# Two transformer blocks on one core: latent and grouped heads of the first mixer divided before their product, and their products written transposed

## What is computed

```python
# 6 latent heads, width 64; 4 differential heads, width 128; 6 grouped heads, width 64
p = softmax(q @ k.T * scale)          # latent and grouped heads: o = p @ v
a = softmax(s0) - lam * softmax(s1)   # differential heads: o = rms_norm(a @ v)
mix = concat([o_latent, o_diff, o_grouped], axis=-1)    # 256 x 1280
x = x + mix @ w_o
```

## Time and profile before

| | before |
|---|---|
| median of 3 runs | 2326.1 us |
| profiled execution | 2325.82 us, of which the span is 2323.9 us |
| TensorE busy | 2224.8 us, 96% |
| VectorE / ScalarE / GpSimd busy | 1693.7 / 1476.0 / 227.8 us |
| mean granted TensorE clock | 0.982 |
| attention steps 8 to 22, first layer | about 105 to 184 us from the span's start |
| the same, second layer | about 472 to 551 us |

### The profile page before, as it was taken

The page is one execution under the profiler, slowest core; times in us unless marked ns, Lnnn a source line. Parts: engine busy times, 40 slices in busy tenths (PEclk is TensorE's granted clock), DMA queues, the critical chain, the costliest instruction groups (busy, mean ns, idle before and its releaser), DMA issues.

```text
span 2323.9 us, 31037 instructions
## 1 busy us (share of the span) xinstructions
PE 2224.8 (96%) x11606; PEld 1882.1 (81%) x11606; DVE 1693.7 (73%) x2409; ACT 1476.0 (64%) x2139; POOL 227.8 (10%) x138
## 2 busy tenths in 40 slices
PE   8889999889999999999999899999999999999997
PEld 7777888787887898788888788888888888888885
DVE  6845556864556546655655699999999999999998
ACT  6654445664444465444466488777878787888886
POOL 1420000331001250100242000000000000000000
PEclk9999999999999999999999799999999999999999
DMA  7425555414554643655544399999999999999996
GB/s 285 136 72 182 189 187 191 151 59 153 189 187 159 213 145 129 207 184 190 200 150 148 110 341 367 351 365 348 366 353 370 350 369 348 370 365 373 367 372 240
DMA packets 157275, 570.89 MB, mean 246 GB/s; under 512 B 18560, under 2 KB 18912, under 8 KB 156480
## 3 DMA queue, kind: packets, MB, share of 16 engines
q1 hardware_dynamic: 154032, 555.58, 67.7%
q0 software_dynamic: 3088, 13.27, 1.6%
HBM read 567.72 MB, written 1.05 MB: 245 GB/s over the span
## 4 chain that ended last, share of the span: by engine, by line
PE 72%; DVE 4%; ACT 1%; issue 1%; POOL 0%; DVEq 0%; POOLq 0%; ACTq 0%
PE bank L500 20%; PE bank L502 19%; PE bank L501 19%; PE bank L2035 3%; PE bank L2036 2%; PE bank L2037 2%; PE bank L1661 1%; DVE w_lo L441 1%; PE bank L1003 1%; PE bank L2601 1%; PE bank L1018 1%; DVE X L1919 1%; PE bank L945 1%; PE bank L2532 0%; DVE X L1878 0%
## 5 line engine op out<-in xcount | busy, mean ns | idle before, releaser
L441 DVE TENSOR_TENSOR w_lo<-raw,w_hi 128x1024 fp32r<-128x1024 f32 x990 | 1193.2, 1224 | 299.0 <-ACT w_hi L435 268.5
L435 ACT CAST w_hi<-raw 128x1024 fp32r<-128x1024 f32 x1055 | 1101.0, 1051 | 321.8 <-PE bank L502 269.1
L500 PE MATMUL bank<-w_hi,x_hi 128*128 128x512 f32 (+2 forms) x2144 | 838.7, 391 | 23.4 <-DVE x_lo L1943 7.9
L502 PE MATMUL bank<-w_hi,x_lo 128*128 128x512 f32 (+2 forms) x2144 | 826.1, 385 | 0.0
L501 PE MATMUL bank<-w_lo,x_hi 128*128 128x512 f32 (+2 forms) x2144 | 825.9, 385 | 0.0
L500 PEld LDWEIGHTS bank<-w_hi,x_hi 128*128 128x128 f32 x2144 | 406.7, 190 | 102.1 <-POOL w_lo L441 8.5
L502 PEld LDWEIGHTS bank<-w_hi,x_lo 128*128 128x128 f32 x2144 | 405.9, 189 | 79.6
L501 PEld LDWEIGHTS bank<-w_lo,x_hi 128*128 128x128 f32 x2144 | 406.9, 190 | 73.3
L441 POOL TENSOR_TENSOR w_lo<-raw,w_hi 128x1024 fp32r<-128x1024 f32 x65 | 154.6, 2382 | 576.4 <-ACT w_hi L435 571.5
L502 PE MATMUL bank<-w_hi,qk_l 128*128 128x512 f32 (+1 forms) x496 | 191.4, 386 | 0.0
L500 PE MATMUL bank<-w_hi,qk_l 128*128 128x512 f32 x448 | 178.1, 398 | 0.3 <-DVE w_lo L441 0.3
(11 more groups left out here) (272 smaller groups left out, 2024.1 us busy)
## 6 DMA issues: line engine op xcount, KB each, us to landing
raw<-in_stream SPq DMA_DIRECT2D x1055, 512.0 KB, 5.7
tab<-in_lngb POOLq DMA_DIRECT2D x5, 1024.0 KB, 7.5
arena<-in_rpb POOLq DMA_DIRECT2D x16, 256.0 KB, 6.5
tab<-in_rowv POOLq DMA_DIRECT2D x2, 640.0 KB, 10.3
X<-in_x SPq DMA_DIRECT2D x1, 1024.0 KB, 5.2
out_y<-X SPq DMA_DIRECT2D x4, 256.0 KB, 2.0
tab<-in_ropec POOLq DMA_DIRECT2D x2, 448.0 KB, 5.3
tab<-in_ropes POOLq DMA_DIRECT2D x2, 448.0 KB, 7.6
```

The lines of the kernel that those rows point to most:

```text
L435: nc.scalar.copy(w_hi[:, s % SPLIT, :], raw[:, slot, :]).then_inc(hi_done, 1)
L441: e.tensor_tensor(w_lo[:, s % SPLIT, :], raw[:, s % RAW, :], w_hi[:, s % SPLIT, :].bitcast(F32), ALU.subtract).then_inc(done, 1)
L500: pe.matmul(out, xh, wh, start=first, stop=False)
L502: return pe.matmul(out, xl, wh, start=False, stop=last)
```

## The change

1. For maps 8 to 19 VectorE divides the exponentials in place, one step after they are made and ahead of the row limit of the next map (`divide`: one reciprocal, two scalings of 128 x 256). TensorE's transposition of such a map waits for that.
2. The products of maps 8 to 19 are made for two maps at once (`column_products`), in steps 12, 14, ..., 22: values stationary (64 columns), PT moving (256 columns), each head into 64 partitions of bank 3. The result is the transposed block already. ScalarE copies it to x_hi in two instructions of 64 x 256, VectorE makes x_lo in two.
3. The scaling into O and the units of blocks 0, 1, 2, 7, 8, 9 are gone.
4. `out_half(7)` moves from step 21 to step 22, and `out_half(8)` from step 22 to behind the loop.

```diff
+            def divide(m):
+                sc2 = slice(2 * (m % 8), 2 * (m % 8) + 2)
+                e.wait_ge(p_ready, E.map.at(m) + 1)
+                E.link(e.reciprocal(rsum[:, sc2], psum_[:, sc2]))
+                for tb in range(TB):
+                    j = 2 * (m % 8) + tb
+                    i = e.tensor_scalar(PP[:, m % 4, tb, :], PP[:, m % 4, tb, :], rsum[:, j:j + 1], None, ALU.mult)
+                i.then_inc(g_divided, 1)
+            def column_products(m):
+                two, p = maps[m - 1:m + 1], columns_up_to(m) // 2 - 1
+                half = slice(p % 2 * S, p % 2 * S + S)
+                g = E.map.at(m - 1)
+                if E.kind == "pe":
+                    e.wait_ge(*copied(m))
+                    e.wait_ge(o_done, g)
+                    for kb in range(TB):
+                        for c, a in enumerate(two):
+                            r = a["block"][1]
+                            i = e.matmul(O_BANK[r * 64:(r + 1) * 64, half], a["v"](kb), PT[:, (m - 1 + c) % 2, kb, :],
+                                         start=kb == 0, stop=kb == TB - 1)
+                            if kb == TB - 1:
+                                i.then_inc(o_full, 1)
+                if E.kind == "act":
+                    e.wait_ge(o_full, g + 2)
+                    for a in two:
+                        k, r = a["block"]
+                        i = nc.scalar.copy(x_hi[r * 64:(r + 1) * 64, k, :], O_BANK[r * 64:(r + 1) * 64, half])
+                    i.then_inc(gt_hi, 1)
+                if E.kind == "dve":
+                    e.wait_ge(gt_hi, E.gd.at(2 * p + 2) // 2)
+                    for a in two:
+                        k, r = a["block"]
+                        rows = slice(r * 64, (r + 1) * 64)
+                        e.tensor_tensor(x_lo[rows, k, :], O_BANK[rows, half], x_hi[rows, k, :].bitcast(F32),
+                                        ALU.subtract).then_inc(o_done, 1)
             for step in range(M + lag + 1):
+                if E.kind == "dve" and 0 < step <= M and "block" in maps[step - 1]:
+                    divide(step - 1)
...
-                        e.wait_ge(p_ready, g + 1)
+                        if "block" in maps[m]:
+                            e.wait_ge(g_divided, E.gd.at(columns_up_to(m)))
+                        else:
+                            e.wait_ge(p_ready, g + 1)
...
-                if 0 <= m < M:
+                if 0 <= m < M and "block" in maps[m] and maps[m]["half"] == 1:
+                    column_products(m)
+                if 0 <= m < M and "block" not in maps[m]:
...
-            def out_half(n):
+            def out_half(n, done=0):
...
+                    if O_ORDER[n] < 3:
+                        e.wait_ge(o_done, E.map.at(2 * DH + 2 * (O_ORDER[n] + 1)))
+                    if O_ORDER[n] >= 7:
+                        e.wait_ge(o_done, E.map.at(done))
...
-                if step == 15:
-                    out_unit(2, 0, 2, 2 * DH + 4)
-                if step == 17:
-                    out_unit(2, 2, 1, 2 * DH + 6)
-                if step == 19:
-                    out_unit(2, 7, 1, 2 * DH + 9)
-                if step == 21:
-                    out_unit(2, 8, 1, 2 * DH + 11)
...
-                if step >= 14:
+                if 14 <= step < 21:
                     out_half(step - 14)
+                if step == 22:
+                    out_half(7, 2 * DH + MH + 4)
...
-            out_unit(2, 9, 1, 0)
+            out_half(8)
             out_half(9)
```

More of the change, by code:

```diff
@@ L402, in build @@
         hs_src, hs_done = sem("hs_src"), sem("hs_done")
+        g_divided, gt_hi = sem("g_divided"), sem("gt_hi")
         og_full, og_done = sem("og_full"), sem("og_done")
@@ L460, in __init__ @@
                 self.hs = Count()
+                self.gd = Count()
                 self.hq = Count()
@@ L786, in copy, with columns_up_to @@
                     e.tensor_copy(PT[:, m % 2, :, :], src).then_inc(pt_dve, 1)
+            def columns_up_to(m):
+                return sum("block" in a for a in maps[:m + 1])
+            def divide(m):
[33 more added lines that the diff above has]
+                                        ALU.subtract).then_inc(o_done, 1)
             values = E.acc.at()
             for step in range(M + lag + 1):
+                if E.kind == "dve" and 0 < step <= M and "block" in maps[step - 1]:
+                    divide(step - 1)
                 m = step - lag
@@ L907, in attention @@
             E.pd.n += sum(not by_act(m) for m in range(M))
+            E.gd.n += columns_up_to(M - 1)
             E.map.n += M
@@ L1477, in units @@
                 if ask:
-                    return step in (15, 17, 19, 21)
+                    return False
                 if 6 <= step < 6 + MH:
@@ L1580, in first_layer @@
                                  v=lambda kb, h=h: KV[:, kb, h * P + MNOPE:(h + 1) * P],
-                                 out=O[:, :, h * MV:(h + 1) * MV]))
+                                 half=h % 2, block=(h * MV // P, h % 2)))
             for i in range(GH):
@@ L1588, in first_layer @@
                                  v=lambda kb, kv=kv: H[:, kb, C_GV + kv * GD:C_GV + (kv + 1) * GD],
-                                 out=O[:, :, MH * MV + DH * DV + h * GD:MH * MV + DH * DV + (h + 1) * GD]))
+                                 half=kv, block=((MH * MV + DH * DV + h * GD) // P, h % 2)))
             attention(E, maps, fill, act_copies=True, units=units, lag=2)
-            out_unit(2, 9, 1, 0)
+            out_half(8)
             out_half(9)
```

## The result

The change made the kernel a little slower: 2330.07 us (median of 20 runs, 2328.93 to 2332.24) against 2326.55 us (20 runs of the kernel before, 2325.57 to 2327.93), ratio 1.0016, 95% interval 1.0009 to 1.0022. The profiled execution took 2330.08 us, its span 2328.2 us, 4.3 us more than before's 2323.9. The prediction said 2323.0 us, 2317 to 2330: wrong in direction, and outside the range by 0.07 us.

The account below looks back on a forecast made before the run. TensorE was taken to bound the span (72%), VectorE steps 8 to 13. Per layer, -5.8 us from step 14 on and +4.25 before it gave -1.55, -3.1 for both: 2323.0 us against the median of 2326.1, range 2317 to 2330.

Parts of the forecast that it names:

- the price of a divide in steps 9 and 10: VectorE in steps 9 and 10: a divide takes 0.73 us, and waits absorb both, so nothing is added.
- part A: Steps 8 to 13 of a layer, VectorE the bound: +4.25 us on the way to step 14's scores, between 2.8 and 5.3.
- A dearer part A: Steps 8 to 13 cost more, up to 5.3 us a layer; chance 0.12 together with waits that move instead of going.
- the gaps that move: From step 14, pair and copy wait for each other: +3.2, net 0, 2326.2 us; 0.12 together with dearer steps 8 to 13.
- The wait on x_hi: Step 12, VectorE from row limit to norm, waiting for ScalarE's copies: 3.26 us instead of 1.20, +2.06 a layer.
- Part B: From step 14 to the last output product, TensorE the bound: -1.5 + 0.2 - 4.5 = -5.8 us a layer.
- Products: TensorE in steps 15 to 20: transpositions and products of two maps fall from 2.48 to 1.98 us, -1.5 us a layer.
- the rival of a cheaper pair: A pair's product costs no more than one map's: 1.3 us a layer more saved, 2320.4 us; chance 0.05.
- Units: TensorE's gaps at the units of O from step 14 on go: -4.5 us a layer, between 3.7 and 5.0.
- Slow clock: Step 14 starts at half clock and now multiplies a pair instead of one map: +0.2 us a layer.
- the slower rival: The wait on x_hi spreads to even steps 16 to 22: +8.2 us a layer, 2339.5 us; 0.12 together with more slow stretches.
- The slow stretch behind the second layer: Behind the second layer's attention, clock 0.83 over 10 us, goes too: -1.7 us more, 2321.3 us; chance 0.18.

Follow-up runs that it names:

- r_nopool: The changed kernel with all low parts of weights in both first mixers made by VectorE and none by GpSimd: 2341.60 us, 1.0063 of before.
- r_div89: The changed kernel with only the scalings of maps 8 and 9 (steps 9 and 10) moved to ScalarE: 2324.25 us, 0.9987 of before.
- r_hifirst: The changed kernel with ScalarE's two copies to x_hi ahead of the exponentials of the same step instead of behind: 2324.82 us, 0.9989 of before.
- r_nodiv: The changed kernel with the two scalings of each divided map left out, reciprocals and signals kept: 2324.35 us, 0.9974 of before.
- r_actdiv: The changed kernel with the scalings on ScalarE at the head of its step, VectorE making only the reciprocal: 2319.34 us, 0.9969 of before.
- r_tt: The changed kernel with one 128 x 512 product with broadcast reciprocals in place of a map's two scalings: 2326.52 us, 0.9998 of before.
- r_late: The changed kernel with each divide on VectorE behind the row limit of its step instead of ahead: 2326.59 us, 0.9991 of before.
- r_acthi: The changed kernel with scalings on ScalarE and the copies to x_hi ahead of the exponentials, both together: 2320.07 us, 0.9971 of before.
- r_grouped: The change made only for the grouped heads (maps 14 to 19), the latent heads as in the kernel before: 2320.18 us, 0.9971 of before.

## Why the prediction was wrong

**The step that failed** is the price of a divide in steps 9 and 10: in its words, "0.3 to 0.4 us is absorbed by a wait for the product of map 6; step 10: VectorE idles over 1 us for the scores, so the divide costs nothing there", with the bound "0.3 us more each at the worst that I saw; in part A GpSimd is nearly idle". A divide was priced at 0.73 us. In these two steps it takes 2.68 us from the start of the reciprocal to the end, and they put 2.23 and 0.85 us on the path: 3.08 of the 3.3 us missing. r_nopool shows whose doing it is, r_div89 how much (2.95 us). The bound for part A, 5.3 us, didn't hold either; 7.5 was measured. "A dearer part A" stood among the prediction's cases, at 0.12 together with the gaps that move, and its reason there was one more instruction of ScalarE, not GpSimd.

"GpSimd is nearly idle" was a mean over a stretch, 1.1 us of 10 in steps 12 and 13. Steps 9 and 10 are not in that stretch. GpSimd of the kernel before makes a low part of a weight in each of them:

```profile
478.06 2.37 POOL L441 TENSOR_TENSOR w_lo<-raw,w_hi 128x1024 fp32r<-128x1024 f32 x1 [3.14 <-ACT w_hi L435]
482.04 2.39 POOL L441 TENSOR_TENSOR w_lo<-raw,w_hi 128x1024 fp32r<-128x1024 f32 x1 [1.61 <-ACT w_hi L435]
```

The trace of the kernel before had the price in two places as well. VectorE's products of 128 x 192 take 1.16 us for four (at 476.49), so 0.58 for two; once in each layer two of them took 2.83 or 2.84, with a low part that started beside them (82.05, 447.77):

```profile
81.83 2.83 DVE L710 TENSOR_TENSOR arena<-arena,tab 128x192 f32<-128x192 f32 x2
```

```profile
82.05 2.39 POOL L441 TENSOR_TENSOR w_lo<-raw,w_hi 128x1024 fp32r<-128x1024 f32 x1 [5.46 <-ACT w_hi L435]
```

And the 0.3 us that I took for the worst case was this pair of scalings in a divide of the second block's mixer, with the low part beside it:

```profile
816.41 0.87 DVE L991 TENSOR_SCALAR PP<-PP,small 128x256 f32<-128x256 f32 x2
```

```profile
814.47 2.40 POOL L441 TENSOR_TENSOR w_lo<-raw,w_hi 128x1024 fp32r<-128x1024 f32 x1 [4.83 <-ACT w_hi L435]
```

The low part ends at 816.87 and the divide at 817.28, 0.41 us behind it: the same as in steps 9 and 10. The pair was only 0.25 us longer because it began 0.46 us before the low part ended. It was a sample of the tail, not a size. A divide that begins early in a low part pays nearly all of its 2.4 us. With the 3.1 us that the two steps were measured to add, the sum of part A is 4.25 + 3.1 = 7.35 us against 7.5 measured, that of both parts +1.55 us a layer, and the time about 2329 us. This puts a measured term in; it is no second forecast.

The Trainium skill, "SBUF — State Buffer" (Terms; SBUF: two separate sides), says that VectorE and GpSimd arbitrate for one pair of ports, that it is locked for a full instruction, and that the loser blocks instead of sharing. The traces agree by the rows above, in the length of the hold; that I hadn't weighed this rule against the change was part of the error.

**Part A, the other terms.** Steps 11, 12 and 13: forecast 0.73 each, measured 0.58, 0.73, 0.73. The wait on x_hi: forecast 2.06 us on top, measured 2.39. From the row limit of step 12 to the norm it takes 3.59 us (499.61 to 503.20), where 3.26 was forecast; 1.79 of it is the wait, about 1.8 as forecast, and 0.91 the two low parts to the next work, where 0.68 was forecast. The first in, first out reading of ScalarE held, and r_hifirst shows the other side: with the copies in front 1.3 us of the wait go.

**Part B.** The sum was near, -5.8 against -6.3 and -5.6, and part of that is luck: two things that I had not counted lie in it, a shorter slow clock and a new wait, and they mostly cancel. What the sum still lacks, some 0.3 us a layer, I can't put down to a term.
- Products: two steps now have 1.60 us for the pair's transpositions and product, and 0.35 for the other transpositions (518.24 to 518.59), 1.95 together; forecast 1.98. The pair's product has 1.01 us of it (523.03 to 524.04; forecast 1.02), so the rival of a cheaper pair is out.
- Units: no wait on a unit's low part is left. Map 19's copy leaves TensorE waiting 0.68 us; forecast was about 0.8.
- Slow clock: TensorE goes back from 1.2 to 2.4 GHz 4.4 us after the first scores of step 14, where it took 6.3 us before, till 507.40. From T to the end of that output product it takes 7.31 us (510.93 to 518.24) instead of 8.00 (501.07 to 509.07): -0.7, where I had +0.2 for the product and the clock. In the first layer the same stretch goes from 8.87 to 7.40 us, -1.5, and that is the 0.7 us by which part B gained more there. No run tests why the clock comes back sooner. The windows on both sides, of the kernel before and of the kernel after (the figure behind the five engines is the granted clock):

```profile
501.07:507.40 6.33, 6.33 (x30) 5.62 (x30) 2.78 (x13) 2.51 (x6) 1.02 (x1) 0.50 0.01 3
507.40:509.07 1.67, 1.67 (x9) 1.31 (x7) 0.00 (x0) 0.00 (x0) 1.35 (x1) 0.97 0.00 0
```

```profile
510.93:515.36 4.43, 4.43 (x25) 2.83 (x25) 3.03 (x13) 0.00 (x0) 0.00 (x0) 0.52 0.00 0
515.36:518.24 2.88, 2.88 (x15) 2.31 (x13) 0.45 (x2) 2.69 (x8) 0.00 (x0) 1.00 0.01 3
```

- A new wait: 1.39 us (1.43 in the first layer) for a divide at 540.33, which I had excluded by 3 us of slack. The slack was counted with divides of 0.7 us; in part B five of them took 2.5 to 2.8. Counted from the start of step 18 (530.22), the divide of map 18 begins at 7.25 us, where I had 5.4, for two held divides stand ahead of it, and it ends at 10.05, where I had 6.1. It is the slower rival in small, with another cause: a divide that ends later than the transposition wants it, once a layer. r_nodiv, r_actdiv, r_tt, r_late, r_hifirst and r_acthi have no such wait in either layer, and r_div89, which leaves part B alone, has it still.

**The slow stretch behind the second layer** did not go. The window, moved by the 4 us that the stretch ends later, has what the earlier trace rows had, 8.50 us of TensorE at a clock of 0.83. That rival (0.18) is out.

```profile
557.00:567.00 10.00, 8.50 (x38) 7.08 (x39) 6.12 (x12) 7.21 (x14) 2.48 (x5) 0.83 0.14 45
```

**What stays open.** The two groups of executions, for one. The +0.5 and +0.6 us outside the two stretches need no cause in the change: ahead of the first A, where eleven of the twelve kernels have the same work in the same order, their profiles lie between 107.2 and 109.3 us, and between the layers between 288.0 and 291.3. Why the clock comes back sooner in step 14 is open too. A kernel of before with nothing but a scaling beside GpSimd was not tried.

## What to carry to other kernels

Before a scaling or a product is put on VectorE with its operands and its result in SBUF, look at what GpSimd does in that very step, not in the mean of a stretch. In this case the price was the operation's duration plus the rest of GpSimd's subtraction, and an engine that works its list off in order hands that on. When one sample of an operation is a little longer than the others, find what stood beside it and where it overlapped, before calling it the worst case. And split a change by what it costs and what it gives: here the grouped heads had most of the gain and the latent heads all of the cost, and half of the change (r_grouped, 0.9971 of before) beats the whole.

## What the hardware showed unexpectedly

- A pair of scalings on VectorE from SBUF to SBUF that meets a subtraction of GpSimd ends 0.40 to 0.42 us behind the subtraction's end, however much of it is left: so do all fourteen long pairs of the changed kernel (480.68 and 486.88 among them), the one at 816.41 before, and r_late's of 1.31 us at 481.93. One product of 512 columns ends 0.54 to 0.55 us behind it (478.98 and 485.32 in r_tt).
- It goes the other way too: where r_tt's product begins 0.01 us ahead of the low part (534.75 and 534.76), the product takes 0.69 us and the low part 2.94 instead of 2.37.
- Row limits, which read a bank, were not held: r_div89's at 479.31 takes 0.48 us inside a low part that runs from 478.84 to 481.22. Nor was the small reciprocal in front of it, from SBUF to SBUF (0.15 us at 478.95). ScalarE's scalings were not held either (0.49 to 0.51 us in all 48).
- The 48 scalings have a median of 0.352 us for 256 columns. Those that are held and those that aren't have the same form, and a product with two tensors in SBUF is held as much as a scaling with one.
